# mLSTM units: weights times values as three fp32r products of high and low parts, and the outputs' transposes moved ahead of the projections

## The chip, the cores and the metric

The kernel runs on one core of a Trainium2 chip. The metric is the device time of one execution in microseconds (us). TensorE (PE) multiplies and transposes, VectorE (DVE) and ScalarE (ACT) work on tiles, GpSimd (POOL) does small odd jobs, SyncE (SP) issues the loads of weights. Each engine runs its own instructions in the order in which they are written and waits on counters that the others raise.

## What is computed

The reference is a chain of two layer stacks over 512 tokens (256 of context, 256 latent) of width 1024. The change touches one mixer of the second stack, an mLSTM with 4 heads, cut here to what matters:

```python
b = jnp.cumsum(lfc, axis=-1)
log_d = jnp.where(causal, b[..., :, None] - b[..., None, :] + lic[..., None, :], -jnp.inf)
m_row = jnp.maximum(log_inter, jnp.max(log_d, axis=-1))
s = jnp.einsum('bhtd,bhsd->bhts', qc, kc) * jnp.exp(log_d - m_row[..., None])
num = inter[..., None] * jnp.einsum('bhtd,bhde->bhte', qc, c_mat) + jnp.einsum('bhts,bhse->bhte', s, vc)
den = inter * jnp.einsum('bhtd,bhd->bht', qc, n_vec) + jnp.sum(s, axis=-1)
h = num / jnp.maximum(jnp.abs(den), jnp.exp(-m_row))[..., None]
```

Two directions are summed, each head is normed by its root mean square, gated and projected back. The kernel has no chunks and no carried state: for 128 tokens at a time it forms the whole row of gated scores over all tokens that they can see, and multiplies it by the values.

## The kernel before

Most of TensorE's work is weights times activations. It is done in three fp32r products: activation high times weight high, high times low, low times high, where "high" is the value rounded to fp32r and "low" the rest. ACT writes the high part of a weight panel (`hi`, line 1215), DVE the low part (`lo`, line 1795). The mLSTM's scores, the product of the weights with the values, and the transposes are whole float32.

`lstm_layer` runs 16 units, `LSTM_UNITS`: 4 heads times 4 tiles of 128 tokens. A unit of tile 0 or 1 sees 256 tokens, one of tile 2 or 3 sees 512. The loop has 19 steps (`i` = 0 to 18), because a unit is spread over several steps:

- step i: PE forms the scores `("qk", i)` (line 1047). DVE multiplies them by the gates of both directions and makes the weights `("w", i)` (lines 2293 to 2305), the part called *combining* below, then prepares the gates of unit i+1 (`gates`, from line 2267), whose exponentials ACT takes (lines 1617, 1620).
- step i+1: PE transposes the weights, `("wT", i)` (line 1062), one 128x128 piece for each 128 tokens seen. ACT copies them to `WT` in SBUF.
- step i+2: PE multiplies `WT` by the values, `("h", i)` (line 1082), 2 or 4 products of 128 x 512. ACT squares the result (line 1650, with the sum kept), POOL takes the root (lines 2463, 2465), DVE scales it into `rst` (line 2321, by the helper at line 1785). This last step is called the *scaling of h(i)*; its end raises `("h", i)`.
- step i+3: PE transposes `rst`, `("hT", i)` (line 1072, 4 pieces), ACT copies it to `hnT`.

The values come from 32 projections `("mv", ...)`, each 24 matmuls of 128 x 256 (lines 660 to 662). `LSTM_PIECES` says how many stand in each step, from 3 down to 0: 3, 2, 0, 3 over and over for the first three heads, then 2, 1, 1, 1 and none. The first of a step stands behind the scores, the others (`left`) behind the weights' transposes. ACT copies each projection to SBUF (`lstm_v`). In a step before a new head, PE also forms the rows of the gates (`gate_rows`, line 1024) behind the weights' transposes.

In one step PE's order is: scores, a projection, transposes of w(i-1), gate rows if any, the other projections, transposes of h(i-3), h(i-2). PSUM has six banks that go round; a bank is taken again when what was in it has been read.

Of the kernel before, what the change touches and what calls it, by code (L numbers as in the profile page):

```python
# [7 lines left out]
F32 = mybir.dt.float32  # L8
BF16 = mybir.dt.bfloat16
F32R = mybir.dt.float32r  # L10
ALU = mybir.AluOpType
# [221 lines left out]
class Done:  # L233
# [6 lines left out]
    def up(self, signal, *names):  # L240
        signal.n += 1
        self.mark(signal, *names)
        return signal.sem, 1
# [58 lines left out]
def program(nc, d, out):  # L302
    with ExitStack() as ctx:
# [9 lines left out]
        def sb(shape, dt=F32, st=None):  # L313
            return (st or ctx).enter_context(nc.sbuf_tensor(name("t"), shape, dt))
# [74 lines left out]
            H = [(sb([128, 8, T], F32R, st), sb([128, 8, T], F32R, st)) for _ in range(2)]  # L389
        zone = sb([128, NZONES])  # L390
        with ExitStack() as mix:
            hnT = sb([128, 16, T], F32, mix)
            with ExitStack() as st:
                lqT, lkT = sb([128, 8, T], F32, st), sb([128, 8, T], F32, st)
                WT = [sb([128, T], F32, st) for _ in range(2)]
                lg = sb([128, 4, 2, 2, 4], F32, st)
                lf, la, lb = (sb([128, 4, 2, 4], F32, st) for _ in range(3))
                Bs = sb([128, 4, 8], F32, st)
                aT = sb([8, T], F32, st)
                sel = [sb([8, 128], F32, st) for _ in range(2)]  # L400
                col = sb([128, 4, 16], F32, st)
                tri = [sb([128, 128], F32, st) for _ in range(2)]
                pre = sb([128, 2, 4, 4], F32, st)
            with ExitStack() as st:
                lYh, lYl = sb([128, 8, T], F32R, st), sb([128, 8, T], F32R, st)
                s1 = [sb([128, T], F32, st) for _ in range(4)]
# [100 lines left out]
        def lstm_v(h, kt):  # L507

            if h == 0:
                return hnT[:, 8 + kt, :]  # L510
            return (lqT if kt < 2 else lkT)[:, 2 * (h - 1) + kt % 2, :]

        def lstm_masks(zf, zb):
            masks = {}
# [31 lines left out]
        def tensor(e):  # L546
# [423 lines left out]
            def lstm_layer():  # L970
# [38 lines left out]
                def project():  # L1009
                    h, a, tile = pieces.pop(0)  # L1010
                    p = at["mv", 2 * h + a]
                    if tile == 0:
                        weights(p)
                    tokens_left(("mv", h, a, tile), p, 0, 256, xa, tile)
                    if tile == 3:
                        used(p)
# [22 lines left out]
                for i in range(19):  # L1039
                    if i < 16:  # L1040
                        h, tile = LSTM_UNITS[i]
                        n = lstm_width(tile)
                        o = bank(("qk", i))
                        if i == 0:
                            e.wait_ge(*done("lstm qk"))
                        for k in range(2):
                            t = e.matmul(o[:, 0:n], lqT[:, 2 * h + k, tile * 128:tile * 128 + 128], lkT[:, 2 * h + k, 0:n],  # L1047
                                         start=k == 0, stop=k == 1)
                        t.then_inc(*up(pe, ("full", ("qk", i))))
                    left = LSTM_PIECES[i]  # L1050
                    if left:
                        project()
                        left -= 1
                    if i in ahead:
                        output_gate(*ahead[i])
                    if 1 <= i < 17:
                        n = lstm_width(LSTM_UNITS[i - 1][1])
                        o = bank(("wT", i - 1))
                        e.wait_ge(*done(("w", i - 1)))
                        x0 = work[:, 2 * ((i - 1) % 2), 0:n]  # L1060
                        for k in range(n // 128):
                            t = e.transpose(o[:, k * 128:k * 128 + 128], x0[:, k * 128:k * 128 + 128], ident)
                        t.then_inc(*up(pe, ("full", ("wT", i - 1))))
                    if i < 15 and LSTM_UNITS[i + 1][1] == 0:
                        gate_rows(LSTM_UNITS[i + 1][0])
                    for _ in range(left):
                        project()
                    if i >= 3:
                        o = bank(("hT", i - 3))
                        e.wait_ge(*done(("h", i - 3)))  # L1070
                        for c in range(4):
                            t = e.transpose(o[:, c * 128:c * 128 + 128], rst[:, c * 128:c * 128 + 128], ident)
                        t.then_inc(*up(pe, ("full", ("hT", i - 3))))
                    if 2 <= i < 18:
                        h, tile = LSTM_UNITS[i - 2]
                        n = lstm_width(tile) // 128
                        o = bank(("h", i - 2))
                        if tile % 2 == 0:
                            e.wait_ge(*done(("v out", h, tile + 1)))
                        e.wait_ge(*done(("WT", i - 2)))  # L1080
                        for k in range(n):
                            t = e.matmul(o, WT[i % 2][:, k * 128:k * 128 + 128], lstm_v(h, k), start=k == 0, stop=k == n - 1)  # L1082
                        t.then_inc(*up(pe, ("full", ("h", i - 2))))
                mark(pe, "lstm end")
                for g in range(2):
# [116 lines left out]
        def scalar(e):  # L1202
# [109 lines left out]
            def out(key, o, i, func=ACT.Copy, *names, scale=1.0):  # L1312

                e.wait_ge(*done(("full", key)))
                e.activation(o, i, func, scale=scale).then_inc(*up(se, ("read", key), *names))  # L1315
# [267 lines left out]
            def lstm_layer():  # L1583
# [21 lines left out]
                def project():  # L1605
                    h, a, tile = pieces.pop(0)
                    if tile == 0 and (h, a) != (3, 1):
                        begin(at["mv", 2 * h + a])
                    key = ("mv", h, a, tile)
                    out(key, lstm_v(h, tile)[:, a * 256:a * 256 + 256], banks(key)[:, 0:256], ACT.Copy, ("v out", h, tile))  # L1610

                def gates(i):
                    n = lstm_width(LSTM_UNITS[i][1])
# [11 lines left out]
                for i in range(19):  # L1625
                    left = LSTM_PIECES[i]
                    if left:
                        project()
                        left -= 1
                    if 1 <= i < 17:  # L1630
                        n = lstm_width(LSTM_UNITS[i - 1][1])
                        if i >= 3:
                            e.wait_ge(*done(("full", ("h", i - 3))))
                        out(("wT", i - 1), WT[(i - 1) % 2][:, 0:n], banks(("wT", i - 1))[:, 0:n], ACT.Copy, ("WT", i - 1))
                    if i < 15:
                        gates(i + 1)
                    for _ in range(left):
                        project()
                    if i == 10:
                        hi_to(at["mv", 7].i)  # L1640
                    if i >= 3:
                        h, tile = LSTM_UNITS[i - 3]
                        key = ("hT", i - 3)
                        out(key, hnT[:, 4 * h:4 * h + 4, tile * 128:tile * 128 + 128], banks(key).rearrange("p (c t) -> p c t", t=128))
                    if 2 <= i < 18:
                        ssc = col[:, (i - 2) % 4, 14:15]
                        e.wait_ge(*done(("full", ("h", i - 2))))
                        if i >= 3:
                            e.wait_ge(*done(("full", ("hT", i - 3))))
                        e.activation(rst[:, :], banks(("h", i - 2)), ACT.Square, scale=512 ** -0.5, accum_out=ssc).then_inc(  # L1650
                            *up(se, ("h mean", i - 2)))
                    if i == 14:
                        hi_to(at["mo", 0].i)
                    if i == 15:
                        hi_to(at["mz", 0].i)
# [117 lines left out]
        def vector(e):  # L1773
# [6 lines left out]
            def tt(o, a, b, op, *names):  # L1780
                e.tensor_tensor(o, a, b, op).then_inc(*up(ve, *names))  # L1781
# [25 lines left out]
            def begin(p):  # L1807
                lo_to(next_weight(p))
# [398 lines left out]
            def lstm_layer():  # L2207
# [68 lines left out]
                def project():  # L2276
                    h, a, tile = pieces.pop(0)
                    if tile == 0 and (h, a) != (3, 1):
                        begin(at["mv", 2 * h + a])

                gates(0)
                for _ in range(3):
                    project()
                for i in range(19):
# [22 lines left out]
                    if left:  # L2307
                        project()
                        left -= 1
                    if i < 15:  # L2310
                        gates(i + 1)
                        if LSTM_UNITS[i + 1][1] == 2 and LSTM_UNITS[i][0] < 3:
                            select(LSTM_UNITS[i][0] + 1)
# [248 lines left out]
```

## Time and profile before

| | us |
|---|---|
| median of 3 runs | 2081.32 |
| lowest and highest | 2077.82, 2081.70 |
| the profiled execution | 2080.26 |
| its span in the trace | 2078.4 |
| the stretch of the 16 units | about 1465 to 1660 of the span |

The profile is of one execution. In the page each engine has its busy time and share; the timeline gives an instruction's start and its length, and runs of equal ones are merged, with their number behind the x. A product in whole float32 stands there as two MATMUL instructions, so x4 of line 1082 is two products. Matmuls are pipelined, so that the time from start to start tells the cost, and not the length. In square brackets stands how long the engine sat idle just before, and which instruction ended that.

### The profile page before, as it was taken

The page shows a single profiled execution, that of the slowest core. Times are in us where ns is not written, and L with a number is a line of the kernel's source. Part 1 is how long each engine was busy: PE and PEld are TensorE (multiplying, and loading weights), DVE is VectorE, ACT ScalarE, POOL GpSimd, SP SyncE. Part 2 cuts the span into 40 slices and gives each one's busy share as a digit, 9 for nine tenths or more (in the row PEclk, how much of TensorE's full clock was granted, in tenths as well). Part 3 has the DMA queues.
Part 4 walks back from the last instruction along what each step waited for, and adds up shares of the span by engine and source line. Part 5 has one row for each costly group of instructions (what it writes and reads, how often), then busy time and mean ns, then how long its engine had stood idle before and what let it go on. Part 6 is the DMA issues. An engine that isn't in the chain of part 4 may idle for free. (4 is left out here: it accounts for less than half of the span.)

```text
span 2078.4 us, 31546 instructions
## 1 busy us (share of the span) xinstructions
PE 2018.7 (97%) x12882; PEld 1678.4 (81%) x12882; DVE 1129.7 (54%) x2231; ACT 904.7 (44%) x1630; POOL 63.3 (3%) x85
## 2 busy tenths in 40 slices
PE   5999999999999999999999999999999999999998
PEld 3888767779777777788789899997877777888777
DVE  4437662446434343566665776642555454345886
ACT  4446762325423131355664555433344332233575
POOL 0000000001000000100000000000000000001000
PEclk8999999999999999999999999999999999999999
DMA  8222015533444444443117555544211243222311
GB/s 305 97 91 97 16 51 195 191 133 121 149 187 191 162 162 180 183 145 117 50 64 253 214 183 183 183 169 162 102 62 41 82 183 128 96 102 81 122 62 42
DMA packets 47104, 277.15 MB, mean 133 GB/s; under 512 B 4464, under 2 KB 12784, under 8 KB 16752
## 3 DMA queue, kind: packets, MB, share of 16 engines
q1 hardware_dynamic: 42080, 266.94, 35.2%
q10 hardware_dynamic: 4736, 7.34, 1.0%
q8 instruction: 103, 1.69, 0.3%
q0 software_dynamic: 144, 0.85, 0.1%
q14 instruction: 41, 0.34, 0.1%
HBM read 273.01 MB, written 2.10 MB: 132 GB/s over the span
## 5 line engine op out<-in xcount | busy, mean ns | idle before, releaser
L579 PE MATMUL ps<-t 128*128 128x512 f32 (+1 forms) x2184 | 757.2, 347 | 4.9 <-DVE t L1795 4.1
L580 PE MATMUL ps<-t 128*128 128x512 f32 (+1 forms) x2184 | 750.0, 343 | 0.0
L581 PE MATMUL ps<-t 128*128 128x512 f32 (+1 forms) x2184 | 750.0, 343 | 0.0
L1795 DVE TENSOR_TENSOR t<-t 128x1024 fp32r<-128x1024 f32 (+2 forms) x370 | 414.4, 1161 | 259.6 <-ACT t L1215 258.8
L579 PEld LDWEIGHTS ps<-t 128*128 128x128 f32 x2184 | 412.3, 189 | 69.5 <-issue 8.2
L1215 ACT ACTIVATE t<-t 128x1024 fp32r<-128x1024 f32 (+2 forms) x378 | 359.5, 999 | 221.0 <-PE ps L581 155.4
L581 PEld LDWEIGHTS ps<-t 128*128 128x128 f32 x2184 | 412.3, 189 | 50.8
L580 PEld LDWEIGHTS ps<-t 128*128 128x128 f32 x2184 | 412.4, 189 | 50.1 <-issue 0.7
L1781 DVE TENSOR_TENSOR t<-t 128x512 f32<-128x512 f32 (+10 forms) x621 | 232.0, 394 | 206.5 <-ACT t L1315 73.2
L1315 ACT ACTIVATE t<-ps 128x512 f32<-128x512 f32 (+1 forms) x244 | 115.6, 493 | 351.7 <-PE ps L581 238.0
L1790 DVE SCALAR_TENSOR_TENSOR t<-ps,t 128x256 f32<-128x256 f32 (+2 forms) x176 | 83.2, 496 | 179.7 <-PE ps L581 159.3
L660 PE MATMUL ps<-t 128*128 128x256 f32 (+1 forms) x524 | 157.9, 301 | 0.5 <-DVE t L1795 0.2
L662 PE MATMUL ps<-t 128*128 128x256 f32 (+1 forms) x524 | 151.4, 289 | 0.0
L661 PE MATMUL ps<-t 128*128 128x256 f32 (+1 forms) x524 | 151.4, 289 | 0.0
L1790 DVE SCALAR_TENSOR_TENSOR t<-t 128x256 f32<-128x256 f32 (+6 forms) x226 | 99.6, 467 | 46.8 <-ACT t L1315 34.2
L660 PEld LDWEIGHTS ps<-t 128*128 128x128 f32 x524 | 99.7, 190 | 8.8 <-issue 3.0
L661 PEld LDWEIGHTS ps<-t 128*128 128x128 f32 x524 | 99.8, 191 | 3.7 <-issue 2.2
L662 PEld LDWEIGHTS ps<-t 128*128 128x128 f32 x524 | 99.8, 190 | 1.4
L1781 DVE TENSOR_TENSOR t<-ps,t 128x128 fp32r<-128x128 f32 (+5 forms) x134 | 52.2, 395 | 87.3 <-ACT t L1674 35.0
L690 PE MATMUL ps<-t 128*32 128x256 f32 x1152 | 73.4, 393 | 21.8 <-DMA t<-in_panels 21.1
L1338 ACT ACTIVATE t<-ps,t 128x512 f32<-128x512 f32 (+1 forms) x128 | 87.0, 696 | 9.7 <-DVE t L1781 9.7
L1252 ACT ACTIVATE t<-t 128x256 f32<-128x256 f32 (+1 forms) x62 | 30.9, 503 | 126.0 <-DVE t L1790 108.9
(166 smaller groups left out, 2072.2 us busy)
## 6 DMA issues: line engine op xcount, KB each, us to landing
t<-in_panels SPq DMA_DIRECT2D x236, 1024.0 KB, 4.8
t<-in_panels SPq DMA_DIRECT2D x19, 512.0 KB, 4.1
t<-in_panels SPq DMA_DIRECT2D x6, 768.0 KB, 4.1
t<-in_window ACTq DMA_DIRECT2D x4, 768.0 KB, 4.3
t<-in_ctxT SPq DMA_DIRECT2D x1, 1024.0 KB, 14.6
t<-in_xT SPq DMA_DIRECT2D x1, 1024.0 KB, 16.7
t<-in_ctxT ACTq DMA_DIRECT2D x1, 1024.0 KB, 5.6
t<-in_xT ACTq DMA_DIRECT2D x1, 1024.0 KB, 7.5
```

What stands on the lines that cost most here:

```text
L579: e.matmul(o, hi[:, k, w], xh[:, c0:c1], start=k == 0, stop=False)
L580: e.matmul(o, hi[:, k, w], xl[:, c0:c1], start=False, stop=False)
L581: t = e.matmul(o, lo[:, k, w], xh[:, c0:c1], start=False, stop=k == p.nk - 1)
L660: e.matmul(o, xh[:, r], hi[:, k, n0:n1], start=k == 0, stop=False)
L661: e.matmul(o, xh[:, r], lo[:, k, n0:n1], start=False, stop=False)
L662: t = e.matmul(o, xl[:, r], hi[:, k, n0:n1], start=False, stop=k == p.nk - 1)
L1215: e.activation(p.half(whi[p.buf], a), p.half(raw[p.slot], a), ACT.Copy).then_inc(*up(se, ("hi", p.i, a)))
L1315: e.activation(o, i, func, scale=scale).then_inc(*up(se, ("read", key), *names))
L1338: e.activation(work[:, 2 * par + g, x * w:x * w + w], banks(("s", s, i, g))[:, x * w:x * w + w], ACT.Exp, scale=sc_, bias=nm[:, c:c + 1], ...
L1781: e.tensor_tensor(o, a, b, op).then_inc(*up(ve, *names))
L1790: e.scalar_tensor_tensor(o, a, s_, b, o1, o2).then_inc(*up(ve, *names))
L1795: e.tensor_tensor(p.half(wlo[p.buf], a), p.half(raw[p.slot], a), p.half(whi[p.buf], a).bitcast(F32), ALU.subtract).then_inc(*up(ve, ("lo", ...
```

## The change

Values and transposed weights are kept in high and low fp32r parts (`lstm_v` and `lstm_vl`, `WTh` and `WTl`). ACT writes the high part, as it wrote the whole before; DVE subtracts it from what is in PSUM and writes the low part, which is new work. On PE each product of line 1082 becomes three. The transposes of h(i-3) go ahead of the remaining projections of their step, on PE and on ACT. A bank with a projection or with transposed weights is now given back by DVE, behind ACT. Buffers lie over one another differently (`tri` over `WTl`), without further work.

```diff
-                    for _ in range(left):
-                        project()
                     if i >= 3:
                         o = bank(("hT", i - 3))
                         e.wait_ge(*done(("h", i - 3)))
...
+                    for _ in range(left):
+                        project()
                     if 2 <= i < 18:
...
-                            t = e.matmul(o, WT[i % 2][:, k * 128:k * 128 + 128], lstm_v(h, k), start=k == 0, stop=k == n - 1)
+                            w = slice(k * 128, k * 128 + 128)
+                            e.matmul(o, WTh[i % 2][:, w], lstm_v(h, k), start=k == 0, stop=False)
+                            e.matmul(o, WTh[i % 2][:, w], lstm_vl(h, k), start=False, stop=False)
+                            t = e.matmul(o, WTl[i % 2][:, w], lstm_v(h, k), start=False, stop=k == n - 1)
...
+                    r = slice(a * 256, a * 256 + 256)
+                    key = ("mv", h, a, tile)
+                    e.wait_ge(*done(("v hi", h, a, tile)))
+                    tt(lstm_vl(h, tile)[:, r], banks(key)[:, 0:256], lstm_v(h, tile)[:, r].bitcast(F32), ALU.subtract,
+                       ("v out", h, tile), ("read", key))
...
+                    if 1 <= i < 17:
+                        n = lstm_width(LSTM_UNITS[i - 1][1])
+                        if i >= 3:
+                            e.wait_ge(*done(("full", ("h", i - 3))))
+                        e.wait_ge(*done(("WT hi", i - 1)))
+                        tt(WTl[(i - 1) % 2][:, 0:n], banks(("wT", i - 1))[:, 0:n], WTh[(i - 1) % 2][:, 0:n].bitcast(F32),
+                           ALU.subtract, ("WT", i - 1), ("read", ("wT", i - 1)))
```

On PE, in step 11 of the kernel before, these rows stand around the weights' transposes (L1062) and the gate rows (L1024); L660 to L662 are projections.

```order
L662 MATMUL ps<-t 128x256
L1062 MATMUL ps<-t 128x128 x4
L1024 MATMUL ps<-t 128x512 x2
L660 MATMUL ps<-t 128x256
L661 MATMUL ps<-t 128x256
```

Two projections (48 rows) later come the transposes of h(8), L1072, h(9), L1082, and the next scores, L1047:

```order
L661 MATMUL ps<-t 128x256
L662 MATMUL ps<-t 128x256
L1072 MATMUL ps<-t 128x128 x4
L1082 MATMUL ps<-t 128x512 x2
L1047 MATMUL ps<-t 128x256 x2
```

In the changed kernel the same step reads as follows (L1072 are now the weights' transposes, L1034 the gate rows, L1080 the transposes of h(8), L670 to L672 projections).

```order
L672 MATMUL ps<-t 128x256
L1072 MATMUL ps<-t 128x128 x4
L1034 MATMUL ps<-t 128x512 x2
L1080 MATMUL ps<-t 128x128 x4
L670 MATMUL ps<-t 128x256
L671 MATMUL ps<-t 128x256
```

The transposes of h(8) come two projections earlier.

On DVE, in step 10 before, the end of combining unit 10 (RECIPROCAL to SCALAR_TENSOR_TENSOR of 128x512) is followed at once by the gates of unit 11 (ISA, L2267).

```order
L2301 RECIPROCAL t<-t 128x1
L1785 TENSOR_SCALAR t<-t 128x512
L1790 SCALAR_TENSOR_TENSOR t<-t 128x512
L2267 ISA t<-ps,t 128x512
L2267 ISA t 128x1
L1787 TENSOR_SCALAR t<-t 128x1
```

In the changed kernel (gates at L2284):

```order
L2323 RECIPROCAL t<-t 128x1
L1802 TENSOR_SCALAR t<-t 128x512
L1807 SCALAR_TENSOR_TENSOR t<-t 128x512
L1798 TENSOR_TENSOR t<-ps,t 128x256
L2284 ISA t<-ps,t 128x512
L2284 ISA t 128x1
L1804 TENSOR_SCALAR t<-t 128x1
```

The low part of w(9), a TENSOR_TENSOR out of PSUM, has come between the two.

## Rows read from the trace of the kernel before

**Rows 1.** The page, busy time, share and instructions of TensorE.
```profile
PE 2018.7 (97%) x12882; PEld 1678.4 (81%) x12882; DVE 1129.7 (54%) x2231; ACT 904.7 (44%) x1630; POOL 63.3 (3%) x85
```

**Rows 2.** Windows, units: length, busy PE, PEld, DVE, ACT, POOL, PEclk, DMA share, GB/s.
```profile
1465.00:1660.00 195.00, 193.18 (x1162) 151.30 (x1159) 107.26 (x361) 75.97 (x179) 12.64 (x32) 1.00 0.19 71
```

**Rows 3.** Timeline of PE, steps 10 and 11: start, length, operation, number, idle before.
```profile
1579.72 1.88 PE L1047 MATMUL ps<-t 128*128 128x512 f32 x4
...
1582.48 0.63 PE L1072 MATMUL ps<-t 128*128 128x128 f32 x4 [0.66 <-DVE t L1785]
1582.94 1.88 PE L1082 MATMUL ps<-t 128*128 128x512 f32 x4
1584.66 1.88 PE L1047 MATMUL ps<-t 128*128 128x512 f32 x4
...
1589.78 1.98 PE L1024 MATMUL ps<-t 8*128 8x512 f32 x4
...
1597.54 0.60 PE L1072 MATMUL ps<-t 128*128 128x128 f32 x4
```

**Rows 4.** Timeline of PE, fp32r products of 128x512 in a row, another stage.
```profile
1442.06 0.40 PE L579 MATMUL ps<-t 128*128 128x512 f32 x1
1442.29 0.40 PE L580 MATMUL ps<-t 128*128 128x512 f32 x1
...
1446.85 0.39 PE L579 MATMUL ps<-t 128*128 128x512 f32 x1
```

**Rows 5.** Groups by shape, DVE: count, busy us, mean ns, idle before.
```profile
L1781 DVE TENSOR_TENSOR t<-ps,t 128x512 f32<-128x512 f32 x32 | 21.9, 688 | 45.0 <-ACT t L1674 35.0 <-PE ps L581 9.9
...
L1781 DVE TENSOR_TENSOR t<-ps,t 128x256 fp32r<-128x256 f32 x8 | 3.3, 419 | 0.0
```

**Rows 6.** Timeline of DVE, steps 10 and 11.
```profile
1581.59 0.75 DVE L1785 TENSOR_SCALAR t<-ps,t 128x512 f32<-128x512 f32 x1 [4.73 <-POOL t L2465]
...
1590.03 2.36 DVE L1795 TENSOR_TENSOR t<-t 128x1024 fp32r<-128x1024 f32 x2 [1.64 <-ACT t L1215]
1593.15 0.75 DVE L1785 TENSOR_SCALAR t<-ps,t 128x512 f32<-128x512 f32 x1 [0.76 <-POOL t L2465]
```

**Rows 7.** Timeline of ACT, step 10.
```profile
1588.95 1.99 ACT L1215 ACTIVATE t<-t 128x1024 fp32r<-128x1024 f32 x2
...
1591.32 0.58 ACT L1650 ACTIVATE t<-ps 128x512 f32<-128x512 f32 x1
```

**Rows 8.** Timeline, steps 3, 7 and 8: gate rows on PE, scalings on DVE.
```profile
1500.85 1.98 PE L1024 MATMUL ps<-t 8*128 8x512 f32 x4
...
1502.18 0.75 DVE L1785 TENSOR_SCALAR t<-ps,t 128x512 f32<-128x512 f32 x1 [2.23 <-POOL t L2465]
...
1545.32 1.98 PE L1024 MATMUL ps<-t 8*128 8x512 f32 x4
...
1546.44 0.75 DVE L1785 TENSOR_SCALAR t<-ps,t 128x512 f32<-128x512 f32 x1 [2.71 <-POOL t L2465]
...
1557.82 0.75 DVE L1785 TENSOR_SCALAR t<-ps,t 128x512 f32<-128x512 f32 x1 [3.02 <-POOL t L2465]
...
1558.97 0.60 PE L1062 MATMUL ps<-t 128*128 128x128 f32 x4
```

**Rows 9.** Timeline, steps 13 to 15: scalings of h(10) and h(12), transposes of h(12).
```profile
1612.49 0.75 DVE L1785 TENSOR_SCALAR t<-ps,t 128x512 f32<-128x512 f32 x1 [5.10 <-POOL t L2465]
...
1630.18 0.75 DVE L1785 TENSOR_SCALAR t<-ps,t 128x512 f32<-128x512 f32 x1 [2.71 <-POOL t L2465]
...
1631.07 0.63 PE L1072 MATMUL ps<-t 128*128 128x128 f32 x4 [0.50 <-ACT t L1215]
```

**Rows 10.** Another stage: a wait of PE, and the busy time and clock behind it.
```profile
1955.81 0.79 PE L642 MATMUL ps<-t 128*128 128x512 f32 x1 [2.38 <-DVE t L1795]
...
1955.60:1959.00 3.40, 3.19 (x8) 2.51 (x9) 3.05 (x7) 1.76 (x3) 0.00 (x0) 0.50 0.25 53
```

More of the change, by code:

```diff
@@ L391, in program @@
         with ExitStack() as mix:
+            with ExitStack() as s2:
+                hnR = sb([128, 16, T], F32R, s2)
             hnT = sb([128, 16, T], F32, mix)
             with ExitStack() as st:
+                with ExitStack() as s2:
+                    lqR, lkR = sb([128, 8, T], F32R, s2), sb([128, 8, T], F32R, s2)
                 lqT, lkT = sb([128, 8, T], F32, st), sb([128, 8, T], F32, st)
-                WT = [sb([128, T], F32, st) for _ in range(2)]
+                WTh = [sb([128, T], F32R, st) for _ in range(2)]
+                with ExitStack() as s2:
+                    tri = [sb([128, 128], F32, s2) for _ in range(2)]
+                WTl = [sb([128, T], F32R, st) for _ in range(2)]
                 lg = sb([128, 4, 2, 2, 4], F32, st)
@@ L401, in program @@
                 col = sb([128, 4, 16], F32, st)
-                tri = [sb([128, 128], F32, st) for _ in range(2)]
                 pre = sb([128, 2, 4, 4], F32, st)
@@ L509, in lstm_v, with lstm_vl @@
             if h == 0:
-                return hnT[:, 8 + kt, :]
-            return (lqT if kt < 2 else lkT)[:, 2 * (h - 1) + kt % 2, :]
+                return hnR[:, 4 + kt, :]
+            return (lqR if kt < 2 else lkR)[:, 2 * (h - 1) + kt % 2, :]
+        def lstm_vl(h, kt):
+            return lstm_v(1, kt) if h == 3 else hnR[:, (12, 8, 12)[h] + kt, :]
         def lstm_masks(zf, zb):
@@ L1609, in project @@
                     key = ("mv", h, a, tile)
-                    out(key, lstm_v(h, tile)[:, a * 256:a * 256 + 256], banks(key)[:, 0:256], ACT.Copy, ("v out", h, tile))
+                    e.wait_ge(*done(("full", key)))
+                    e.activation(lstm_v(h, tile)[:, a * 256:a * 256 + 256], banks(key)[:, 0:256], ACT.Copy).then_inc(
+                        *up(se, ("v hi", h, a, tile)))
                 def gates(i):
@@ L1633, in lstm_layer @@
                             e.wait_ge(*done(("full", ("h", i - 3))))
-                        out(("wT", i - 1), WT[(i - 1) % 2][:, 0:n], banks(("wT", i - 1))[:, 0:n], ACT.Copy, ("WT", i - 1))
+                        e.wait_ge(*done(("full", ("wT", i - 1))))
+                        e.activation(WTh[(i - 1) % 2][:, 0:n], banks(("wT", i - 1))[:, 0:n], ACT.Copy).then_inc(
+                            *up(se, ("WT hi", i - 1)))
                     if i < 15:
                         gates(i + 1)
+                    if i >= 3:
+                        h, tile = LSTM_UNITS[i - 3]
+                        key = ("hT", i - 3)
+                        out(key, hnT[:, 4 * h:4 * h + 4, tile * 128:tile * 128 + 128], banks(key).rearrange("p (c t) -> p c t", t=128))
                     for _ in range(left):
@@ L1640, in lstm_layer @@
                         hi_to(at["mv", 7].i)
[L1641 to L1644, printed above, removed]
                     if 2 <= i < 18:
@@ L2309, in lstm_layer @@
                         left -= 1
+                    if 1 <= i < 17:
+                        n = lstm_width(LSTM_UNITS[i - 1][1])
+                        if i >= 3:
+                            e.wait_ge(*done(("full", ("h", i - 3))))
+                        e.wait_ge(*done(("WT hi", i - 1)))
+                        tt(WTl[(i - 1) % 2][:, 0:n], banks(("wT", i - 1))[:, 0:n], WTh[(i - 1) % 2][:, 0:n].bitcast(F32),
+                           ALU.subtract, ("WT", i - 1), ("read", ("wT", i - 1)))
                     if i < 15:
```

## The prediction

> **What bounds the kernel now.** I read the page first: TensorE is busy for 97% of the span, 2018.7 us [rows 1], and no other engine comes near. Then I read the stretch that the change touches, the 16 mLSTM units, by windows: 193.18 us of PE in 195.00, at the full clock of 2.4 GHz (PEclk 1.00), with DVE at 107.26 and ACT at 75.97 [rows 2]. So PE sets the time there, instruction by instruction, and an edit to PE's work counts in full as long as the others keep up. Averages do not say whether they do. For this I followed the timeline of the units: where in each step PE takes up a result of DVE, and how early that result is. In step 10 PE already waits 0.66 us for the scaling of h(7) [rows 3]; everywhere else in the loop, but for step 15 [rows 9], the projections that stand ahead of the outputs' transposes cover DVE's, ACT's and POOL's chain.
>
> **Part 1, the products.** The x4 of line 1082 takes from 1582.94 to 1584.66, 1.72 us for two whole-float32 products, 0.86 each [rows 3]. A head has 2 + 2 + 4 + 4 of them, the four heads 48. The nearest row for the new ones has exactly their shape: an fp32r product of 128 x 512 follows the one before after 0.23 us; 21 of them, from 1442.06 to 1446.85, take 4.79, 0.228 each [rows 4]. Three make 0.68, weight loads included. PE saves 0.86 - 0.68 = 0.18 on each, 0.35 on an h of two pieces, 0.71 on one of four, and 48 x 0.177 = **8.5 us** in all. Worst case, with 0.24 a product, it would be 6.7.
>
> The Trainium skill, "FP8 and Floating Point Precision", section "TensorE Precision Notes", says that true FP32 takes four passes through the array. The row agrees in kind (0.86 is four times 0.215). By passes alone, three for four, the saving would be 48 x 0.215 = 10.3 us; the measured fp32r step is a little longer than a pass, so the rows' 8.5 goes into the sum.
>
> **Part 2, the low parts on DVE.** 32 subtractions of 128 x 256 out of PSUM into fp32r last 0.42 us each (the second of [rows 5], the same form); of the 16 for the weights, 8 have 256 columns and 8 have 512, 0.42 and 0.69 [rows 5]. DVE's instructions overlap by some 0.08, so I take 0.34 and 0.61 in a queue. The sum of lengths is 40 x 0.42 + 8 x 0.69 = 22 us on an engine with 88 us free [rows 2]. As a share this costs nothing. But DVE works in order, and some of the 22 us lie ahead of the scaling that PE waits for. ACT's work stays what it was: the high part costs what the whole copy did. Banks come free later, by DVE's lag, but each is taken again only six takes later, a whole step or more; I found none that would come late.
>
> **Part 3, the move.** PE now wants h(i-3) ahead of the remaining projections. In steps 3, 7 and 11 that is two projections, some 5.8 us, earlier; in steps 4, 8 and 12 the same; in 5 and 9 one projection. The cover of the chain is gone there. The chain: combining, low part of w, gates of the next unit (DVE), their exponentials (ACT), ACT's square of h, POOL's root, DVE's scaling. Place by place, where "ready" is the scaling's start + 0.75 + 0.14 (as from 1581.59 to 1582.48 [rows 3, 6]):
>
> - Step 3: gate rows end at 1502.83, h(0) is ready at 1503.07 [rows 8]; the wait would be 0.24 by the move alone. One low part of w more in the chain (0.34) and PE earlier by h's 0.35 make **0.9**.
> - Step 7: gate rows end at 1547.30, h(4) is ready at 1547.33 [rows 8]. With the same two terms **0.7**.
> - Step 8: from scaling to scaling DVE took 1557.82 - 1546.44 = 11.38; a low part of values (0.34) and one of w (0.61) make it 12.33. PE's way from the end of the gate rows to that of the weights' transposes, 1558.97 + 0.60 - 1547.30 = 12.27, loses 0.36 by h(5) and is 11.9 [rows 8]. That is a wait of 0.4, and as lengths run some 0.2 into the next instruction I take **0.6**. Step 4 has the same pattern, 0.6.
> - Step 10: nothing stands between, the wait of 0.66 stays, for its whole chain shifts with h(7).
> - Step 11: gate rows end at 1591.76, h(8) is ready at 1593.15 + 0.89 = 1594.04 [rows 3, 6]. This one is late since ACT rounds a weight panel (1.99 us) ahead of its square and DVE subtracts one (2.36) [rows 6, 7]. 2.28 by the move alone, + 0.34 + 0.35: **3.0**. In the kernel before two projections hide it, up to 1597.54 [rows 3].
> - Steps 13 to 15: here one projection a step is left, nothing to move, but DVE's chain already binds: PE waits for h(12) at 1631.07, ready then to the hundredth (1630.18 + 0.89) [rows 9]. From the scaling of h(10) to that of h(12), 17.69 us, come four low parts of 0.34 to 0.42, 1.4 to 1.5 us. PE, which would arrive earlier, waits the more: **2.5** beyond what it waits now.
> - After it the chain has slack again; the panel for the output gate may come 0.3 late.
>
> **The sum.** Saved 8.5. New waits 0.9 + 0.6 + 0.7 + 0.6 + 3.0 + 2.5 + 0.3 = 8.6. The two cancel: **+0.1 us**. A check as a balance: h(0) to h(7) save 4.2, waits take 2.8, lead 1.4; h(8) saves 0.35 inside the 3.0, so behind by 1.2 at step 11; h(9), h(10) give 1.1; the DVE chain puts the transposes of h(12) 1.5 late; h(13) to h(15) give back 1.8. Within half a us of zero.
>
> **The clock.** In another stage PE sat idle 2.38 us, and the next eight matmuls, which take 0.23 each at 2.4 GHz, took 3.4 us at a PEclk of 0.50, 1.2 GHz [rows 10]: 3.4 - 8 x 0.227 = 1.6 us lost. In the units' stretch PE never idled over 0.7 us in a row and the clock stayed whole. The waits in step 11 (3.0) and in step 15 (2.5 + 0.7) are longer than the one that a fall followed. I count one such fall, +1.6; bounds none and two, 0 and 3.3. The Trainium skill, "TensorE: Matmul & The Clock Gate", section "Why this matters for your kernels", asks to avoid idle gaps of PE between bursts of matmuls, since the clock falls behind them; this is the page's rule against this change, and rows 10 show a case of it.
>
> Together +0.1 + 1.6 = +1.7 on the profiled execution's 2080.26, so 2082.0. The median of before is 1.1 above the profiled one, so by the median it is 2083.0; I forecast **2082.5**, between the two.
>
> **The rivals.** *The cover holds* (faster): if the scaling were ready each time when PE comes, all 8.5 us stay, 2072. For it: DVE is idle 88 us of the stretch, and it sits idle 2 to 5 us ahead of most scalings [rows 6, 8, 9]. Against it: that idle time is waiting within the same chain, for ACT's square and POOL's root, and steps 7 and 11 show the result late or just in time even without the new work. Half of it (low parts cheaper, shorter handovers) would give 2076 to 2077. *DVE's chain becomes the bound* (slower): the place is steps 11 and 12 to 15. If a low part holds DVE's queue for 0.5 us and not 0.34 (it waits for ACT's high part first), the 11 that lie in the chains above add 0.15 each, 1.7 us, and both long waits drop the clock, 3.3: 2080.3 + 0.1 + 1.7 + 3.3 = 2085.4, 2086.5 by the median. It decides from a low part of about 0.5 us in the queue on. *The trio isn't cheaper than one float32 product*: it needs 0.29 per fp32r product; the 0.228 [rows 4] speaks against it, chance 1 in 50, inside the third case.
>
> **How the numbers follow.** The forecast's case, the gain eaten by waits with none or one fall of the clock, 0.62; its own range 2079.5 to 2085. The cover holds at least in half, 0.16. DVE's chain binds harder, 0.22. A measurement of this kernel can tell about 0.2%, 4.2 us, from no change: 2077.2 to 2085.5. Faster by more needs over half of the gain: 0.14. Slower by more is most of the third case and the edge of the first: 0.20. Same: 0.66. For 8 in 10 the range reaches half into either rival: 2076.5 to 2087.
>
> **What would show it.** In the trace of the changed kernel: lines 1093 to 1095 at 0.227 from start to start, 144 of them, shows part 1 right. PE idle ahead of line 1080 in steps 3, 4, 7, 8 (under 1 us each), 11 (3) and 15 (3) shows parts 2 and 3 right; no idle there, and a loop of 187 us, shows the cover. A PEclk under 1.00 in the units' stretch shows the fall. DVE's line 1798 out of PSUM over 0.45 us for 256 columns would speak for the slower case. What would make the whole wrong is a chain that I followed with a wrong order: a low part that waits for ACT where I took it as ready, or a bank that comes free late.

## The result

The changed kernel took 2085.36 us (median of 19 runs, 2081.57 to 2088.87), the kernel before 2080.61 in the same sessions (19 runs, 2077.06 to 2083.38). The ratio is 1.0025, 95% interval 1.0019 to 1.0032: slower by 5.2 us by this ratio (4.0 to 6.7); the plain medians lie 4.8 apart. The forecast was 2082.5 with a range up to 2087, so the time lies inside the range, but on the side to which I had given one chance in five. One execution of a later kernel, trio_stay, took 3333 us and is left out of that kernel's ratio.

### The profile page after: what moved, and what is told of

The parts are those of the page before. It is cut to its first block and busy times, and to the rows that moved or that the text cites. A ratio compares the mean times of both kernels' runs of the same rounds, so it can differ in the third digit from the quotient of the medians.

```text
span 2086.2 us, 31704 instructions
## 1 busy us (share of the span) xinstructions
PE 2022.1 (97%) x12930; PEld 1694.9 (81%) x12930; DVE 1148.2 (55%) x2279; ACT 904.7 (43%) x1630; POOL 63.8 (3%) x85
## 5 line engine op out<-in xcount | busy, mean ns | idle before, releaser
L1328 ACT ACTIVATE t<-ps 128x512 f32<-128x512 f32 (+1 forms) x196 | 98.0, 512 | 311.9 <-PE ps L591 238.5
L670 PE MATMUL ps<-t 128*128 128x256 f32 (+1 forms) x524 | 160.2, 306 | 0.4 <-DVE t L1812 0.2
L671 PE MATMUL ps<-t 128*128 128x256 f32 (+1 forms) x524 | 153.7, 293 | 0.0
L672 PE MATMUL ps<-t 128*128 128x256 f32 (+1 forms) x524 | 153.6, 293 | 0.0
L1798 DVE TENSOR_TENSOR t<-ps,t 128x256 fp32r<-128x256 f32 (+6 forms) x182 | 72.8, 412 | 101.5 <-ACT t L1691 34.9
L670 PEld LDWEIGHTS ps<-t 128*128 128x128 f32 x524 | 102.1, 195 | 6.5 <-DVE t L1802 2.1
L672 PEld LDWEIGHTS ps<-t 128*128 128x128 f32 x524 | 102.1, 195 | 1.4
## 6 DMA issues: line engine op xcount, KB each, us to landing
t<-in_xT SPq DMA_DIRECT2D x1, 1024.0 KB, 17.1
```

The costliest lines, as they stand in the source:

```text
L670: e.matmul(o, xh[:, r], hi[:, k, n0:n1], start=k == 0, stop=False)
L671: e.matmul(o, xh[:, r], lo[:, k, n0:n1], start=False, stop=False)
L672: t = e.matmul(o, xl[:, r], hi[:, k, n0:n1], start=False, stop=k == p.nk - 1)
```

## The profile after

The page of the changed kernel says of its engines what [rows 1] says of before:

```profile
PE 2022.1 (97%) x12930; PEld 1694.9 (81%) x12930; DVE 1148.2 (55%) x2279; ACT 904.7 (43%) x1630; POOL 63.8 (3%) x85
```

PE has 48 instructions more (144 trio products for 96 halves), DVE 48 more: the low parts. PE's busy time went up by 3.4 us in all, although the products became cheaper. But ahead of the loop, in work that did not change, it is 4.6 us more in this profile (1424.2 for 1419.6); in the loop it fell, by 1.5 (192.1 for 193.6) and not by the 8 that the products save. The windows show what took the rest; first the whole stretch of the units, then four pieces of it (columns as in [rows 2]):

```profile
1467.00:1668.00 201.00, 192.01 (x1212) 166.45 (x1209) 126.19 (x409) 76.05 (x179) 13.12 (x32) 0.96 0.19 69
1506.67:1510.09 3.42, 3.42 (x18) 3.42 (x17) 3.17 (x8) 0.00 (x0) 0.00 (x0) 0.50 0.00 0
1551.05:1554.46 3.41, 3.41 (x19) 3.41 (x18) 3.17 (x9) 0.00 (x0) 0.00 (x0) 0.50 0.00 0
1595.42:1602.25 6.83, 5.17 (x25) 5.20 (x26) 5.58 (x19) 0.00 (x1) 0.65 (x2) 0.50 0.44 156
1639.79:1643.21 3.42, 3.42 (x10) 2.64 (x9) 3.14 (x10) 1.72 (x4) 0.42 (x2) 0.50 0.27 57
```

Against [rows 2], 195 us at a PEclk of 1.00, it is 201 us at 0.96: in four places the granted clock was 0.50, 1.2 GHz. Each stands at one of PE's longer waits: in steps 3, 7 and 15 just behind it, in step 11 from 1.7 us before its end on. The timeline of PE in steps 3, 6, 7, 11 and 15 (L1034 gate rows, L1080 transposes of h(i-3)):

```profile
1502.50 1.98 PE L1034 MATMUL ps<-t 8*128 8x512 f32 x4
1505.39 0.63 PE L1080 MATMUL ps<-t 128*128 128x128 f32 x4 [0.91 <-DVE t L1802]
...
1540.32 0.63 PE L1080 MATMUL ps<-t 128*128 128x128 f32 x4 [0.66 <-DVE t L1802]
...
1549.96 0.63 PE L1080 MATMUL ps<-t 128*128 128x128 f32 x4 [0.69 <-DVE t L1802]
...
1591.87 1.98 PE L1034 MATMUL ps<-t 8*128 8x512 f32 x4
1597.08 1.09 PE L1080 MATMUL ps<-t 128*128 128x128 f32 x4 [3.23 <-DVE t L1802]
...
1638.97 0.63 PE L1080 MATMUL ps<-t 128*128 128x128 f32 x4 [2.83 <-DVE t L1802]
```

L1802 is DVE's scaling of h. The wait of 0.66 in step 6 was there before too (as in [rows 3] for step 10, and both are unchanged); the others are new, or, in step 15, grew from 0.50 [rows 9]. In step 11 one sees the chain of [rows 6] and [rows 7] on DVE and ACT, in the same order and nearly the same lengths, now with nothing on PE to cover it:

```profile
1588.50 0.42 DVE L1798 TENSOR_TENSOR t<-ps,t 128x256 fp32r<-128x256 f32 x1
...
1593.06 2.36 DVE L1812 TENSOR_TENSOR t<-t 128x1024 fp32r<-128x1024 f32 x2 [2.12 <-ACT t L1228]
1596.18 0.75 DVE L1802 TENSOR_SCALAR t<-ps,t 128x512 f32<-128x512 f32 x1 [0.77 <-POOL t L2494]
```
```profile
1591.98 1.99 ACT L1228 ACTIVATE t<-t 128x1024 fp32r<-128x1024 f32 x2
1593.88 0.58 ACT L1667 ACTIVATE t<-ps 128x512 f32<-128x512 f32 x1
```

The low part of w(9) is the first row. The panel (1.99 us on ACT) and then the square stand behind it, then POOL, then the scaling at 1596.18.

**The account of the loop**, from the first gate rows to the transposes of h(15): 195.28 us before (1465.13 to 1660.41), 201.08 after (1467.11 to 1668.19), so 5.8 more. The products: on PE an h of two pieces (six products for two) takes 1.38 us for 1.72, one of four pieces 2.75 for 3.43, 8 x 0.34 + 8 x 0.68 = 8.2 saved. The waits: 9.0 us in sum for 1.8, 7.2 lost. The clock: the two projections behind the wait of step 3 take 7.3 us for 5.8, in step 7 the same, 3.0 together; in step 11 transposes and projections take 0.74 + 7.77 for 0.38 + 5.83, 2.3; behind step 15 ten products take 3.96 from start to start, for 2.41 behind the wait of the same step in trio_stay (below), where the clock stayed whole: 1.5. That is 6.8. And -8.2 + 7.2 + 6.8 = +5.8, as seen. The rest of the difference between the two spans (2086.2 and 2078.4) stands before the loop, in work that did not change.

## The experiments

The table has them all: the loop's length, PE's waits in it (idle of 0.12 us or more, summed), how long the clock stood at 1.2 GHz in it, and the ratio of times to the kernel before, with its 95% interval. Loop, waits and clock are of one profile each.

| kernel | loop us | waits us | at 1.2 GHz us | ratio (interval) |
|---|---|---|---|---|
| before | 195.3 | 1.8 | 0 | 1 |
| changed | 201.1 | 9.0 | 17.1 | 1.0025 (1.0019 to 1.0032) |
| changed_again | 198.9 | 9.8 | 10.2 | 1.0022 (1.0013 to 1.0031) |
| trio_stay | 190.6 | 4.9 | 0 | 0.9983 (0.9974 to 0.9992) |
| move_only | 200.9 | 4.8 | 6.8 | 1.0028 (1.0017 to 1.0038) |
| no_low | 195.9 | 6.9 | 10.2 | 1.0005 (0.9995 to 1.0014) |
| panel_behind | 197.7 | 6.5 | 13.7 | 1.0000 (0.9991 to 1.0009) |
| one_between | 192.7 | 5.4 | 3.4 | 0.9986 (0.9977 to 0.9995) |
| rows128 | 198.3 | 10.3 | 6.8 | 1.0017 (1.0008 to 1.0026) |
| rows128_again | 198.3 | 10.4 | 6.8 | 1.0020 (1.0011 to 1.0028) |
| stay_late | 190.4 | 4.1 | 0 | 0.9979 (0.9969 to 0.9989) |
| pieces | 186.9 | 1.3 | 0 | 0.9956 (0.9942 to 0.9970) |
| before_pieces | 192.9 | 0 | 0 | 0.9976 (0.9966 to 0.9986) |

### The move undone: trio_stay

```diff
+                    for _ in range(left):
+                        project()
                     if i >= 3:
                         o = bank(("hT", i - 3))
...
-                    for _ in range(left):
-                        project()
```

and the same on ACT.

> The changed kernel with the move alone undone: on PE and on ACT the transposes of h(i-3) stand behind the remaining projections again; trios and low parts stay. My theory: the loss of the change (+5.2 us against the kernel before) is PE waiting for h in steps 3, 7, 11 and 15 and the clock that falls behind these waits, and the move is what uncovers steps 3, 7 and 11. Then the 0.9 and 0.8 us waits of steps 3 and 7 and the 3.3 of step 11 go (some 1 us may come up in steps 6, 10 and 14, which have no projection), the wait of step 15 stays near 3: 8.5 saved, 5.5 to 6 of new waits, 0 to 2 of clock, so 3 us faster to 1 us faster than the kernel before. Rival: the low parts on DVE are the whole cause and the place of the transposes does not matter; then it stays 4 to 6 us slower.

It is 3.5 us faster than the kernel before (1.7 to 5.4), and the loop 4.7 shorter, more than I expected. The rival, which put the whole loss on the low parts, is out. The waits of steps 3, 4, 7, 8 and 11 are gone. Of the small ones that I expected elsewhere only one came up, 0.65 us in step 14; steps 6 and 10 keep their 0.66. The long one of step 15 is left:

```profile
1628.13 0.63 PE L1082 MATMUL ps<-t 128*128 128x128 f32 x4 [2.95 <-DVE t L1802]
...
1625.00:1635.00 10.00, 7.05 (x34) 5.76 (x33) 7.35 (x18) 6.99 (x14) 1.56 (x4) 1.00 0.29 105
```

The second row is the window around it: here the clock did not fall (1.00), though the wait is as long as that of step 15 in the changed kernel, behind which it fell.

### The move alone: move_only

The kernel before, with the transposes of h ahead of the remaining projections on PE and ACT.

> The kernel before with the move alone: whole float32 products, no low parts, but the transposes of h(i-3) ahead of the remaining projections on PE and ACT. My theory: waits of about 0.2 us in steps 3 and 7 and of 2.3 us in step 11 come up, 2 to 2.7 us in all, and the clock falls behind the last one (1.5 to 2.3 us): 3.5 to 5 us slower than before, if it falls in steps 3 and 7 too up to 7. Rival, the move is free as long as there are no low parts: no difference within 1 us.

5.8 us slower (3.5 to 7.9), a little more than expected, with 5.6 of it in the loop. PE waits 0.25 us in step 3, where the sum had said 0.24, and 2.77 in step 11, where it had said 2.3; the two new waits are 3.0 us, and the clock that falls behind the second is the rest:

```profile
1595.73 0.66 PE L1070 MATMUL ps<-t 128*128 128x128 f32 x2 [2.77 <-DVE t L1785]
...
1594.80:1601.60 6.80, 5.87 (x28) 5.90 (x29) 5.51 (x21) 1.45 (x5) 0.00 (x0) 0.50 0.43 154
```

So whatever the trios and low parts do, the move by itself costs as much as the whole change shows.

### No low parts: no_low

```diff
-                            e.matmul(o, WTh[i % 2][:, w], lstm_vl(h, k), start=False, stop=False)
-                            t = e.matmul(o, WTl[i % 2][:, w], lstm_v(h, k), start=False, stop=k == n - 1)
+                            e.matmul(o, WTh[i % 2][:, w], lstm_v(h, k), start=False, stop=False)
+                            t = e.matmul(o, WTh[i % 2][:, w], lstm_v(h, k), start=False, stop=k == n - 1)
```

and both subtractions off DVE, so that the low parts are left out of the result.

> The changed kernel without the low parts' subtractions on DVE: PE still issues three products each, all of them with the high parts, so the weights times values are computed to fp32r's precision alone; banks are given back by ACT. My theory: DVE's chain gets shorter by 0.34 to 1 us a step, so the waits of steps 4 and 8 are none, of 3 and 7 about 0.4, of 11 about 2.5 to 3, of 15 about 1.5: 8.5 saved against 4.5 of waits, and the clock still falls behind step 11 at least (2 us) and perhaps behind 15: 0 to 2.5 us faster than the kernel before. Rival, it is the three products themselves that cost more than the timeline's steps say: it stays 3 us or more slower.

1.0 us slower than before (between 1.0 faster and 2.9 slower), where 0 to 2.5 faster was expected. Only the edge of the interval reaches into that. The waits came as expected: 0.58 in step 3, 0.38 in step 7, none in 4 and 8, 1.53 in step 15, and in step 11 hardly less than with the low parts:

```profile
1593.06 1.09 PE L1080 MATMUL ps<-t 128*128 128x128 f32 x4 [3.09 <-DVE t L1802]
```

Missed was the clock, which stood at 1.2 GHz for 10.2 us of the loop, also behind the wait of only 0.38 us in step 7. The low parts account for 0.3 us of wait in steps 3 and 7 each and for 1.3 in step 15, as the sum had them (0.34 a part), and for 0.14 of the largest wait, where the sum had 0.34.

### The panel behind the square: panel_behind

```diff
                     if 2 <= i < 18:
                         ssc = col[:, (i - 2) % 4, 14:15]
...
+                    if i == 10:
+                        hi_to(at["mv", 7].i)
```

with the same line gone from its place ahead, and likewise for DVE's low part.

> The changed kernel with one thing moved: the high and low parts of the weight panel that ACT and DVE make in step 10 stand behind ACT's square and DVE's scaling of h(8), no longer ahead of them. It measures by itself the largest wait of the changed kernel, 3.3 us ahead of the transposes of h(8) in step 11. My theory, that ACT's 1.99 us for the panel stands in the chain to that wait: it falls to 0.8 to 1.5 us, some of the gain comes back as a wait in step 12 (up to 0.8), and the fall of the clock there is shorter (3.4 us in place of 6.8, 0.8 to 1.6 us of time): 2 to 3.5 us faster than the changed kernel, that is 2 to 3 us slower than the kernel before. Rival, the wait comes from DVE's combining and gates, which are unchanged: no difference to the changed kernel.

It is as fast as the kernel before (within 1.9 us), and by the two ratios some 5 us faster than the changed one, more than the 2 to 3.5 expected; its loop is 3.4 shorter. The wait of step 11 is what steps 3 and 7 have:

```profile
1592.83 1.09 PE L1080 MATMUL ps<-t 128*128 128x128 f32 x4 [0.70 <-DVE t L1802]
```

2.5 us of the 3.23 were the panel. No wait came up in step 12. The clock fell in all four places here too, for 3.4 us each; behind step 11 for half as long.

### One projection as cover: one_between

```diff
+                    if left == 2:
+                        project()
+                        left -= 1
                     if i >= 3:
                         o = bank(("hT", i - 3))
```

on PE and on ACT.

> The changed kernel with one projection put back ahead of the transposes of h(i-3) in steps 3, 4, 7, 8 and 11, which have two to place; the second stays behind them. It asks how much cover the chain needs: one projection is 2.9 us. My theory: the waits of 0.7 to 1 us in steps 3 and 7 go, that of step 11 goes from 3.3 to 0.4, steps 4 and 8 have none; what is left is the 0.66s of steps 6 and 10 and the 3 of step 15, the same as with the move undone in whole: 2 to 4.5 us faster than the kernel before. Rival, that the distance between the transposes of h and the next h counts too, because ACT takes the transposes' copy ahead of its square: 0 to 2 us slower than with the move undone, near the kernel before.

2.9 us faster than before, as expected, within the interval of trio_stay. The waits of steps 3, 4, 7, 8 are gone, that of step 11 is 0.17. The loop is 2.0 us longer than with the move undone in whole: the waits are 0.5 more in sum (one of 0.98 in step 12 is new, the 0.65 of step 14 is gone), and behind step 15 the clock fell for 3.4 us.

The wait of step 12 is not the rival's. Step 12 has one projection left, and the condition `left == 2` leaves it behind the transposes. The first three rows are of one_between, the others of trio_stay, which has that projection ahead: the scalings of h(8) and h(9), then the transposes of h(9).

```profile
1593.36 0.75 DVE L1808 TENSOR_SCALAR t<-ps,t 128x512 f32<-128x512 f32 x1 [0.77 <-POOL t L2500]
1603.39 0.75 DVE L1808 TENSOR_SCALAR t<-ps,t 128x512 f32<-128x512 f32 x1 [1.10 <-POOL t L2500]
1604.29 0.63 PE L1083 MATMUL ps<-t 128*128 128x128 f32 x4 [0.98 <-DVE t L1808]
```
```profile
1589.37 0.75 DVE L1802 TENSOR_SCALAR t<-ps,t 128x512 f32<-128x512 f32 x1 [0.77 <-POOL t L2494]
1599.39 0.75 DVE L1802 TENSOR_SCALAR t<-ps,t 128x512 f32<-128x512 f32 x1 [1.53 <-POOL t L2494]
1602.19 0.60 PE L1082 MATMUL ps<-t 128*128 128x128 f32 x4
```

From scaling to scaling it is 10.03 and 10.02 us, so the distance between the transposes of h and the next h did not lengthen the chain here. In trio_stay PE comes at 1602.19 for a result that is ready at 1600.28; without the projection of 2.9 us ahead it would have waited 1.0.

### The gate rows over the whole array: rows128, changed_again, rows128_again

```diff
-                aT = sb([8, T], F32, st)
-                sel = [sb([8, 128], F32, st) for _ in range(2)]
+                aT = sb([128, T], F32, st)
+                sel = [sb([128, 128], F32, st) for _ in range(2)]
```

with zeros in the further rows.

> The changed kernel with the gate rows multiplied over all 128 rows of the array instead of 8 (the other 120 rows are zero on both sides, one memset of 128x512 more on DVE), the same number of columns and the same time on PE. In the changed kernel the clock fell to 1.2 GHz behind waits of only 0.98 and 0.76 us in steps 3 and 7, where the gate rows stand just ahead of the wait and transposes around it. Theory A: the clock goes by how much of the array works, and 8 rows of 128 count as hardly any, so that 2 us of gate rows and the wait act as one idle stretch; then the falls of steps 3 and 7 are gone here, the one of step 11 is shorter, and the kernel is 3 to 4 us faster than the changed one. Theory B: only idle time counts, and the falls come where they came: no difference to the changed kernel within 1 us.

The first profile looked like theory A: no fall in steps 3 and 7, in spite of waits of 1.10 and 0.89 (0.91 and 0.69 in the changed kernel, which the expectation gives as 0.98 and 0.76), and 3.4 us at 1.2 GHz in step 11 in place of 6.8. The time was 3.5 us over the kernel before, against 5.2 of the changed one, which was timed in other sessions. So both ran again, side by side.

> The changed kernel as it is, again, to stand on one chip with the next run. Two things are asked of it: whether the falls of the clock behind the waits of steps 3, 7, 11 and 15 come again in a second profile (I expect at least three of the four places), and its time beside the next kernel's: 1.0020 to 1.0032 of the kernel before.

> The changed kernel with the gate rows over all 128 rows of the array, again, beside the unchanged one. In its first profile the falls of steps 3 and 7 were gone and that of step 11 was half as long, and the loop took 198.3 us against 201.1. Theory A (8 busy rows of 128 count to the clock as nearly idle): this again, and 1.5 to 3 us less than the run before this one. Theory B (the first profile was chance, the falls depend on when they are looked at): falls in steps 3 or 7 here too, and no difference in time beyond 1 us.

The times are 1.0022 and 1.0020, the medians 1.1 us apart: no difference clear of the noise, though one of 1.5 us, the least that theory A expected, is not ruled out. And in its second profile the changed kernel has no falls in steps 3 and 7 either, with the same waits:

```profile
1506.00:1512.00 6.00, 6.00 (x45) 5.69 (x44) 5.79 (x15) 0.60 (x2) 0.00 (x0) 1.00 0.14 38
1550.00:1556.00 6.00, 6.00 (x44) 5.63 (x43) 5.73 (x14) 0.85 (x3) 0.00 (x0) 1.00 0.27 66
1591.20:1598.00 6.80, 4.26 (x20) 4.29 (x21) 5.61 (x16) 0.77 (x3) 1.44 (x2) 0.50 0.43 157
```

I had expected at least three of the four falls; two came, those behind the long waits. In steps 4 and 8, where the first profile has no wait, this one has 0.38 and 0.36: where PE runs at full clock it catches up with DVE's chain again, and a wait takes back a part of what the clock would have taken. So the loops differ by 2.1 us and not by the 3.0 of two falls. Theory A is not shown. What repeated in both pairs is step 11 alone: 6.8 us at 1.2 GHz with 8 rows and 3.4 with 128. Whether the rows cause this stays open: in steps 3 and 7 two profiles of the very same kernel differ, and in panel_behind step 11 had 3.4 with 8 rows, behind a shorter wait.

### Towards a faster version: stay_late, pieces, before_pieces

stay_late is trio_stay with the low part of the weights behind the gates on DVE:

```diff
-                    if 1 <= i < 17:
-                        n = lstm_width(LSTM_UNITS[i - 1][1])
...
                     if i < 15:
                         gates(i + 1)
...
+                    if 1 <= i < 17:
+                        n = lstm_width(LSTM_UNITS[i - 1][1])
```

> The changed kernel with the move undone, and with the low part of the transposed weights on DVE behind the gates of the next unit, no longer ahead of them. With the move undone alone the loop took 190.6 us against 195.3 before, with one long wait left, 2.95 us in step 15. My theory, that each low part ahead of the gates lengthens the chain to h by its own 0.34 to 0.61 us: two such parts leave the chain of steps 13 to 15, the wait of step 15 falls to 2.2, the rest stays hidden as it was: 0.7 to 1 us faster than with the move undone alone, 4 to 6 us faster than the kernel before. Rival, a bank that comes free later by this (the transposed weights' is given back by DVE) makes PE wait elsewhere and eats it: no faster than with the move undone alone.

The wait of step 15 fell from 2.95 to the 2.20 expected:

```profile
1628.78 0.63 PE L1082 MATMUL ps<-t 128*128 128x128 f32 x4 [2.20 <-DVE t L1802]
```

But waits of 0.39 and 0.18 us for projections' banks came up in steps 4 and 8, as the rival has it, and the loop is 0.3 us shorter, not 0.7. With 0.9979 it can't be told from trio_stay's 0.9983.

pieces adds another spread of the projections:

```diff
-LSTM_PIECES = [3, 2, 0, 3, 3, 2, 0, 3, 3, 2, 0, 3, 2, 1, 1, 1, 0, 0, 0]
+LSTM_PIECES = [3, 1, 1, 3, 3, 1, 1, 3, 3, 1, 1, 2, 2, 1, 2, 1, 0, 0, 0]
```

> As the one before (move undone, low part of the weights behind the gates), and the projections spread more evenly over the steps: 3, 1, 1, 3 in place of 3, 2, 0, 3 for a head, and 2, 2, 1, 2, 1 in place of 3, 2, 1, 1, 1 in steps 11 to 15. This puts one projection on PE into steps 6 and 10, which have none and where PE waits 0.66 us each also in the kernel before, and two into step 14, ahead of the wait of step 15. My theory, that all waits of the loop are waits for a chain of 7 to 11 us that projections can cover: the 0.66s go, the wait of step 15 falls to 1 or under: 6.5 to 8.5 us faster than the kernel before. Rival, waits for banks and for the weight panels take their place: 5 us or less.

> The kernel before with that same spread of the projections and nothing else. It says how much of the last kernel's gain belongs to the spread: by my theory the two waits of 0.66 us and the 0.5 of step 15, 1.3 to 1.8 us faster than the kernel before; a spread that brings the whole gain of the last kernel would show 5 us or more.

pieces is 9.2 us faster than the kernel before (6.2 to 12.1), more than expected, and beats both kernels. The stretch of its units, and below it that of the kernel before with the same spread:

```profile
1465.50:1652.40 186.90, 185.47 (x1213) 160.40 (x1210) 126.01 (x409) 75.57 (x179) 12.68 (x32) 1.00 0.20 74
```
```profile
1463.60:1656.50 192.90, 192.90 (x1165) 151.79 (x1162) 107.25 (x361) 76.56 (x179) 13.35 (x32) 1.00 0.20 72
```

The first loop is 8.4 us shorter than before, with 1.3 us of waits left, one of 0.74 for a bank and one of 0.58 in step 15. The second is 2.4 us shorter with no wait at all. So in the loop the spread brings 2.4 and the trios, once covered, 6.0 more (8.2 less 1.3 of waits would be 6.9; no wait in the brackets accounts for the 0.9 between). In time before_pieces gained 5.0 (2.9 to 7.1), more than the 1.3 to 1.8 expected and more than its loop shows. Its profile is 5.4 us shorter than that of before: 2.4 in the loop, 1.5 in the first 60 us of the program, where nothing changed, and 1.5 behind the loop, where the fall of the clock in the attention stage [rows 10] is missing. That fall is missing in pieces and panel_behind too, and one of the two profiles of the kernel with the gate rows over the whole array has it and the other has not (rows128, then rows128_again):

```profile
1961.70:1965.00 3.30, 3.30 (x9) 2.56 (x9) 2.88 (x8) 1.36 (x3) 0.00 (x0) 0.50 0.46 107
```
```profile
1961.90:1965.30 3.40, 3.21 (x14) 2.64 (x15) 3.05 (x7) 1.74 (x3) 0.00 (x0) 1.00 0.33 67
```

So it comes and goes with nothing changed. Whether it was missing in the other executions of before_pieces as well, and how much of its 5.0 us is the spread's, stays open.

## Why the prediction came out as it did

**The products** (8.5): right. 8.2 us by the trace; a trio of 128 x 512 takes 0.68 to 0.69 us. no_low and trio_stay have the same steps.

**The low parts on DVE**: right in size, and in what they add to the waits (0.33 and 0.31 in steps 3 and 7, no_low). 0.418 us for 256 columns (40 of them) and 0.681 for 512 (8), in the groups of the changed kernel's stretch, where the sum had 0.42 and 0.69:

```profile
L1798 DVE TENSOR_TENSOR t<-ps,t 128x256 fp32r<-128x256 f32 x40 | 15.9, 418 | 13.8 <-ACT t L1624 13.8
...
L1798 DVE TENSOR_TENSOR t<-ps,t 128x512 fp32r<-128x512 f32 x8 | 5.5, 681 | 0.5 <-ACT t L1650 0.5
```

DVE also sat idle 13.8 us ahead of the 40, for ACT's high parts. The prediction had this in its slower rival alone; by no_low it did not lengthen the waits beyond the 0.34 a part.

**The waits** (8.6 new): right in place and nearly in size, 7.2 in the first profile of the changed kernel and 8.0 in the second. Step by step, predicted against the two profiles: step 3, 0.9 against 0.91 and 0.92; step 4, 0.6 against none and 0.38; step 7, 0.7 against 0.69 and 0.70; step 8, 0.6 against none and 0.36; step 11, 3.0 against 3.23 twice; step 15, 2.5 beyond the 0.5 against 2.33 and 2.37; behind it, 0.3 against none. move_only shows what of this the move costs by itself, no_low what the low parts add. Two readings of the prediction were wrong without touching its sum: step 6 waits 0.66 in the kernel before, like step 10, and step 12 has one projection left to move, not two.

**The clock** (1.6): this term failed. I had counted one fall, with none and two as bounds, by the one row in which a fall followed a wait [rows 10]. The first profile has four places and the second two, and in step 11 the fall is 6.8 us long and not 3.4: 6.8 and 3.6 us of time lost. I took it for granted that a wait under 1 us, like the 0.66s of before [rows 3], is harmless. Behind the 0.66s no fall came in any profile. Behind 0.91 and 0.69 in steps 3 and 7 it fell in one profile of the changed kernel and not in the other, in panel_behind in both steps, and in no_low behind 0.38. In these steps the weights' transposes and the gate rows stand ahead of the wait and h's transposes behind it; in steps 6 and 10 the scores stand close ahead. Whether that decides it, no run shows. The Trainium skill, "TensorE: Matmul & The Clock Gate", section "Why this matters for your kernels", warns of long idle gaps between bursts of matmuls. The falls at steps 11 and 15 of the changed kernel agree with it; but here falls came behind waits of 0.38 to 0.91 us too, and none behind one of 2.95 (trio_stay), and the measurement decides. With the falls that came in place of the one, the prediction's own sum gives +3.7 by the second profile and +6.9 by the first, where 5.2 was measured over all runs.

**The sign**: with 8.5 against 8.6 I forecast no change, and the clock was to decide. The forecast was 1.2 to 1.7 us of loss, the measured one 5.2. In the first profile the clock cost 5.2 more than its 1.6, and the waits 1.4 less than their 8.6: that the second error made up for a part of the first was luck. The range held the time because it took in two falls. The slower rival was the one that came closest, but by its second half: the low parts did not cost more than 0.34 in the queue, both long waits did drop the clock. The rival in which the cover holds needed what the move took away; with the move undone (trio_stay) and the projections spread (pieces) the loop came down to its 187 us, but 2.4 of that is the spread's own.

## What to carry to other kernels

An instruction that waits for a long chain over other engines is cheap where much independent work stands ahead of it; before moving it forward, read from the timeline when its input is ready and when the engine would arrive. A saving on the bounding engine shortens its own cover too, so it has to come with new cover: here the same trios came with a loss of 5.2 us, a gain of 3.5 or, with an even spread, their part of 9.2, by the order of the rest alone. And a wait of the matmul engine has to be counted with the clock behind it, which can cost as much as the wait.

## What the runs showed of the hardware

- The granted clock fell to 1.2 GHz behind waits of 0.91 and 0.69 us (first profile of the changed kernel) and of 0.38 us (no_low, step 7), and did not behind 2.95 us (trio_stay), nor behind the same 0.92 and 0.70 in changed_again. One profile of a kernel does not say which of its waits drop the clock.
- At 1.2 GHz the 128-column float32 transposes are slow as well: four of line 1080 take 0.74 us from start to start of what follows, 0.38 at 2.4 GHz.
- A whole-float32 product of 128 x 512 took 0.86 us, as two instructions; three fp32r products 0.68 to 0.69. Between transposes and products of either kind the timelines show no gap for the switch.
